# Expert blocks in an order that the chip makes from the token counts, with the second blocks of the two largest experts run on weights still in the ring

## The chip, the cores and the metric

The kernel runs on one core of a Trainium2 chip. The metric is the device time of one execution, in microseconds (us); lower is better. The engines are named as in the profile: PE is TensorE (PEld its weight loads), DVE is VectorE, ACT is ScalarE, POOL is GpSimd, SP is SyncE, which here only issues transfers.

## The reference

A two-part transformer stack over 512 tokens of width 1024, all in float32. The last layer but the final norm is a mixture of experts, and only that part is touched:

```python
def moe_ffn(x, router_w, router_b, w_gu, b_gu, w_down, b_down):
    logits = (xt @ router_w + router_b).astype(jnp.float32)
    top_logits, top_idx = lax.top_k(logits, TOP_K)          # 4 of 32 experts for each token
    gates = jax.nn.softmax(top_logits, axis=-1)
...
        hmid = xt[tok] @ w_gu[e] + b_gu[e]                   # 1024 -> 2048
        glu = jnp.minimum(hmid[:, 0::2], SWIGLU_LIMIT)
        lin = jnp.clip(hmid[:, 1::2], -SWIGLU_LIMIT, SWIGLU_LIMIT)
        act = glu * jax.nn.sigmoid(SWIGLU_ALPHA * glu) * (lin + 1.0)
        return act @ w_down[e] + b_down[e]                   # 1024 -> 1024
...
    y = jnp.einsum("tk,tkd->td", gates.astype(x.dtype), y_slots[slot_of].reshape(n_tok, TOP_K, D))
```

With the inputs of this case the reference's router sends these numbers of tokens to experts 0 to 31 (sum 2048):

```
13 29 105 42 49 66 34 31 44 103 152 37 130 40 66 84 39 41 111 31 98 32 45 50 71 49 124 86 55 57 103 31
```

Thirteen experts have more than 64 tokens. Two have more than 128: expert 10 (152) and expert 12 (130).

## The kernel before

Everything up to the router is a long unrolled program and stays as it is. What follows is `experts`: routing (`out_norm_and_route`), then `first_blocks`, `extra_blocks` and `combine_and_finish`, each a block in which the five engines run their own streams and which ends with a barrier.

**A step of `first_blocks`** handles up to 128 tokens of one expert, and there are 32 steps, j = 0 to 31, in the order of the expert's number. The token rows are fetched by index (POOL, `fetch_rows`), turned by PE (`turn_rows`: the first half before the activations are turned, the second half after), multiplied into the up weights, activated on DVE and ACT, turned again and multiplied into the down weights. ACT stores the result to `expert_rows`. PE ends a step with `find_tokens` (L3559), which prepares the step three later; its row in the trace marks the end of a step.

There are three ways to do the arithmetic. With 64 tokens or fewer a step is **half** (`up_half`, `down_half`): plain float32 matmuls with 64 columns of weights of PE, two of them side by side. With more it is **parted** (`up_parted`, `down_parted`): ACT rounds each weight quarter to its high part, DVE makes the low part, and three fast products replace the float32 one; the low part is written over the weights in the ring (`T.w_low[slot]`), so the weights are used up. Only step 0 can be done **whole** (`up`, `down`): plain float32 matmuls with 128 columns. Which branch is taken is read on each engine from the count of the step (`is_half`, a register loaded from memory, L4198).

**Weights.** An expert has six units of 2 MB: four of the up matrix, two of the down matrix. They lie in a ring of eight slots; SP issues the load of a unit as soon as the unit that had its slot is used (`unit_used`, L4183), so at most one and a third experts are ahead.

**The loop.** Steps 0 to 3 and 28 to 31 are written out, steps 4 to 27 are a hardware loop of six rounds of four steps (`in_rounds`, `Fori` at L4166).

**Second blocks.** If an expert has more than 128 tokens, the rest are done in `extra_blocks`, a loop over 15 possible blocks of which `count` are taken (two here). Each loads its expert's six units again, except that the first one's are issued at the end of `first_blocks` (L4194). It selects its rows from all 512 with 64 matmuls (`gather`, L3665) and then does a half or whole block. DVE finds which experts need one (`Extras.find`, `find_jumps`, `fill`, `find_rows`), in `first_blocks` during steps 0 to 3.

`combine_and_finish` then fetches four result rows for each token (POOL, L4666), sums them with the gates, norms and stores.

Of the kernel before, what the change touches and what calls it, by code (L numbers as in the profile page):

```python
# [5 lines left out]
ALU = mybir.AluOpType  # L6
# [8 lines left out]
P = 128  # L15
# [1006 lines left out]
def mlp(k, i, gain, clear_rows=False):  # L1022
# [15 lines left out]
    with ExitStack() as ctx:  # L1038
# [19 lines left out]
        with k.block() as block:  # L1058
# [35 lines left out]
            def _(act):  # L1094
                if clear_rows:
                    act.wait_ge(k.pool_made.sem, k.pool_made.at(1))
                for n, (u, is_up, j) in enumerate(order):
                    k.round_unit(act, u + 1)
                    if clear_rows:
                        rows = k.rows[3 * n:min(3 * n + 3, BLOCKS)].rearrange("b p d -> p b d")  # L1100
                        act.dma_start(rows, zero[:, :, :].broadcast_to([P, rows.shape[1], D])).then_inc(k.rows_cleared, 16)
# [2362 lines left out]
BLOCKS = EXPERTS + MOST_EXTRA  # L3464
# [3 lines left out]
SLOTS = 8  # L3468

# [32 lines left out]
class Experts:  # L3502


    def __init__(self, k, name, tables, one_by_one):
# [6 lines left out]
        self.loaded = [signal(f"loaded{r}") for r in range(SLOTS)]  # L3512
        self.sel_ready = signal("sel_ready")
        self.index_full = signal("index_full")
        self.index_ready = signal("index_ready")
        self.fetched = [signal(f"rows_fetched{r}") for r in range(2)]
# [16 lines left out]
    def make_sel(self, dve, j, par):  # L3533
# [4 lines left out]
        for t in range(TT):  # L3538
            ins = dve.tensor_scalar(T.sel[:, par, t, :], T.iota[:, :], T.place[:, t, bass.ds(j, 1)], None, ALU.is_equal)
# [95 lines left out]
    def save_act(self, act, j):  # L3635
        k, T = self.k, self.tables
        act.wait_ge(self.act_turned, 2 * j + 2)
        act.activation(T.actT[:, :, :].rearrange("p (b f) s -> p b (f s)", b=2), k.psum[:, 4:6, :], ACT.Copy)\
           .then_inc(self.actT_ready, 2)
# [33 lines left out]
    def up(self, pe, j, home, xg, par):  # L3673

        k, T = self.k, self.tables
        for pair in range(2):
            for r in range(2):
                w = home.wait(pe, 2 * pair + r)
                for g in range(2):
# [4 lines left out]
                    for c in range(HALF_K):  # L3684
                        pe.matmul(bank, xg[:, HALF_K * r + c, :], w[:, c, g * 512:(g + 1) * 512],
                                  start=(r == 0 and c == 0), stop=False)
# [101 lines left out]
    def down(self, pe, j, home, par):  # L3788
        k, T = self.k, self.tables
        self.wait_for_down(pe, j)  # L3790
        for r in range(2):
            w = home.wait(pe, 4 + r)
            for half in range(2):
                bank = k.psum[:, 6 + half, :]
                cols = slice(half * 512, (half + 1) * 512)
                for c in range(HALF_K):
                    pe.matmul(bank, T.actT[:, HALF_K * r + c, :], w[:, c, cols], start=(r == 0 and c == 0), stop=False)
# [207 lines left out]
def experts(k):  # L4005

    with ExitStack() as ctx:
# [3 lines left out]
        T.place = k.sb("moe_place", [P, TT, BLOCKS], ctx=ctx)  # L4011
        T.iota = k.sb("moe_iota", [P, P], ctx=ctx)
# [5 lines left out]
        T.count = k.sb("moe_count", [P, EXPERTS], I32, ctx=ctx)  # L4018
# [7 lines left out]
        T.index = k.sb("moe_index", [P, EXPERTS], I32, ctx=ctx)  # L4026
# [9 lines left out]
        with ExitStack() as inner:  # L4036
# [21 lines left out]
            first_blocks(k, base, T, extras, later)  # L4058
# [4 lines left out]
class Extras:  # L4063
# [4 lines left out]
    def __init__(self, k, T, ctx):  # L4068
        self.k, self.T = k, T
        self.known = k.ctx.enter_context(k.nc.semaphore("extras_known"))  # L4070
        self.flag = k.sb("extra_flag", [P, ROUNDS - 1, EXPERTS], ctx=ctx)
# [18 lines left out]

    def find(self, dve):
# [5 lines left out]
        step(ins)  # L4097
        dve.memset(self.zero[:, :], 0.0)
# [18 lines left out]
    def fill(self, dve, t):  # L4117
# [5 lines left out]
        k.dve.step(dve, self.look_up(dve, self.cand[:, 0], T.place[:, t, EXPERTS:BLOCKS]))  # L4123

    def find_jumps(self, dve):
# [5 lines left out]
        step(dve.tensor_tensor(self.jump[:, 1, :], order[:, 0, :], T.ids[:, :], ALU.subtract))  # L4131
        step(dve.tensor_scalar(self.jump[:, 1, :], self.jump[:, 1, :], float(EXPERTS - 1), float(P), ALU.add, ALU.mult))
        step(dve.tensor_tensor(self.jump[:, 2:, :], order[:, 1:, :], order[:, :-1, :], ALU.subtract))
# [19 lines left out]
def first_blocks(k, E, T, extras, later):  # L4153
# [3 lines left out]
    PER_ROUND = 4  # L4157
    rounds = EXPERTS // PER_ROUND
    k.unit_rounded.passed(len(k.units))
    k.unit_split.passed(len(k.units))  # L4160
    with k.block() as block:
        def in_rounds(eng, step):

            for b in range(PER_ROUND):
                step(0, b, b, True, False)
            with eng.Fori(1, rounds - 1) as i:  # L4166
                for b in range(PER_ROUND):
                    step(i, b, PER_ROUND * i + b, False, False)
            for b in range(PER_ROUND):
                step(rounds - 1, b, PER_ROUND * (rounds - 1) + b, False, True)  # L4170

        @block.sync
        def _(sp):
            def step(i, b, j, first, last):
                if last and b == PER_ROUND - 1:
                    return
# [565 lines left out]
```

## Time and profile before

| what | value |
|---|---|
| median of 3 runs | 3099.53 us (3092.92 to 3102.09) |
| time of the profiled execution | 3098.87 us |
| its span, first to last instruction | 3097.1 us |
| mean granted TensorE clock | 0.935 of full speed |
| `first_blocks` from PE's first expert matmul to its last (1894.2 to 2948.3) | 1054.1 us |
| `extra_blocks`, from there to PE's last expert matmul (3044.1) | 95.8 us |
| from there to the end | 53.0 us |

A time in the trace is a start in us from the span's start, then a duration. "Idle before" in brackets is how long the engine stood still ahead of the row, and what released it; "issue" there means that nothing in the profile was waited for. A row of a queue (PEldq, ACTq, DVEq, SPq) is work of the engine's sequencer, not of the engine.

### The profile page before, as it was taken

How to read it: one execution, taken by the hardware profiler on the slowest of the kernel's cores; microseconds unless marked ns; L12 is line 12 of the kernel's file. 1: busy time of each engine (PE TensorE's matmuls, PEld its weight loads, DVE VectorE, ACT ScalarE, POOL GpSimd, SP SyncE). 2: the span in 40 equal slices, each digit the busy share in tenths (PEclk: the TensorE clock that was granted, in tenths of full speed). 3: DMA queues.
4: the chain of work that ended last, by engine and by line, in shares of the span. 5: the costliest groups of instructions: out<-in, count | busy, mean ns of one | idle time of the engine just before them, and what ended most of it. 6: DMA issues, size and time to landing. Idle time of an engine off the chain costs nothing. (4 is left out here: it accounts for less than half of the span.)

```text
span 3097.1 us, 35668 instructions
## 1 busy us (share of the span) xinstructions
PE 2741.5 (89%) x13162; PEld 1970.5 (64%) x13163; DVE 1614.4 (52%) x2447; ACT 1047.0 (34%) x1464; POOL 193.8 (6%) x213
## 2 busy tenths in 40 slices
PE   7877999999999899999966876998989998899962
PEld 6655778888878788888754663553655455455530
DVE  4864545444555544446855536652855454464413
ACT  4444443322224432233333231330634233343301
POOL 0530000000000000000012130000000000000002
PEclk9988999999999999999976787999999999999986
DMA  3110314444233132322210038999999999999974
GB/s 131 58 51 28 109 62 177 171 169 183 101 120 111 66 116 82 109 82 71 103 60 1 1 122 329 404 414 414 413 385 380 361 412 370 414 412 395 415 291 151
DMA packets 192096, 638.46 MB, mean 206 GB/s; under 512 B 12413, under 2 KB 18204, under 8 KB 191522
## 3 DMA queue, kind: packets, MB, share of 16 engines
q1 hardware_dynamic: 173856, 579.61, 48.7%
q10 hardware_dynamic: 11106, 39.11, 3.2%
q0 software_dynamic: 6912, 16.68, 1.4%
q8 instruction: 151, 2.47, 0.3%
q14 instruction: 71, 0.58, 0.1%
HBM read 600.61 MB, written 43.25 MB: 208 GB/s over the span
## 5 line engine op out<-in xcount | busy, mean ns | idle before, releaser
L91 DVE TENSOR_TENSOR unit_low<-unit_whole,unit_high 128x4096 fp32r<-128x4096 f32 (+3 forms) x95 | 287.8, 3035 | 174.8 <-ACT unit_high L88 172.9
L669 PE MATMUL psum<-tokens_high,unit_high 128*128 128x512 f32 (+2 forms) x1016 | 372.5, 367 | 4.4 <-PEq L865 1.6
L669 PE MATMUL psum<-tokens_high,unit_low 128*128 128x512 f32 (+2 forms) x1016 | 368.7, 363 | 0.0
L669 PE MATMUL psum<-tokens_low,unit_high 128*128 128x512 f32 (+2 forms) x1016 | 368.6, 363 | 0.0
L88 ACT ACTIVATE unit_high<-unit_whole 128x4096 fp32r<-128x4096 f32 (+2 forms) x65 | 225.8, 3474 | 374.2 <-PE psum L669 291.3
L91 DVE TENSOR_TENSOR moe_low<-ring_slot,moe_w_high 128x1024 fp32r<-128x1024 f32 x228 | 266.7, 1219 | 19.4 <-ACT moe_w_high L88 18.4
L88 ACT ACTIVATE moe_w_high<-ring_slot 128x1024 fp32r<-128x1024 f32 x228 | 236.5, 1055 | 61.4 <-PE psum L3875 60.4
L3698 PE MATMUL psum<-ring_slot,hT 128*64 128x512 f32 x1136 | 251.9, 594 | 0.0
L669 PEld LDWEIGHTS psum<-tokens_high,unit_high 128*128 128x128 f32 (+1 forms) x1016 | 191.0, 188 | 37.9 <-DVE unit_low L91 4.0
L669 PEld LDWEIGHTS psum<-tokens_low,unit_high 128*128 128x128 f32 (+1 forms) x1016 | 191.1, 188 | 31.6 <-issue 1.6
L669 PEld LDWEIGHTS psum<-tokens_high,unit_low 128*128 128x128 f32 (+1 forms) x1016 | 191.0, 188 | 30.6 <-issue 0.2
L669 PE MATMUL psum<-unit_high,hidden_high 128*128 128x512 f32 x512 | 199.7, 390 | 0.0
L669 PE MATMUL psum<-unit_high,hidden_low 128*128 128x512 f32 x512 | 199.4, 389 | 0.0
L669 PE MATMUL psum<-unit_low,hidden_high 128*128 128x512 f32 x512 | 199.4, 389 | 0.0
L3741 DVE TENSOR_SCALAR moe_glu<-psum 128x256 f32<-128x256 f32 x42 | 17.8, 425 | 324.4 <-PE psum L3704 232.7
L3698 PEld LDWEIGHTS psum<-ring_slot,hT 128*64 128x64 f32 x1136 | 83.5, 137 | 148.9 <-issue 147.7
L3726 PE MATMUL psum<-ring_slot,moe_actT 128*64 128x512 f32 x640 | 155.8, 641 | 9.7 <-ACT moe_actT L3766 9.7
L1147 DVE TENSOR_TENSOR x_residual<-psum,x_residual 128x512 f32<-128x512 f32 x128 | 84.4, 687 | 117.7 <-PE psum L669 117.7
L3870 PE MATMUL psum<-moe_w_high,moe_xg_high 128*128 128x512 f32 x312 | 131.1, 420 | 0.0
L3755 ACT ACTIVATE moe_sig<-moe_glu 128x256 f32<-128x256 f32 x42 | 17.5, 416 | 316.0 <-DVE moe_glu L3741 316.0
L3871 PE MATMUL psum<-moe_low,moe_xg_high 128*128 128x512 f32 x312 | 122.1, 391 | 0.0
L1137 DVE SCALAR_TENSOR_TENSOR hT<-psum,hidden_relu 128x512 f32<-128x512 f32 x64 | 43.8, 689 | 147.3 <-ACT hidden_relu L1109 147.3
(646 smaller groups left out, 4908.9 us busy)
## 6 DMA issues: line engine op xcount, KB each, us to landing
ring_slot<-in_moe_w_gu SPq DMA_DIRECT2D x118, 2048.0 KB, 19.4
ring_slot<-in_moe_w_down SPq DMA_DIRECT2D x60, 2048.0 KB, 20.5
unit_whole<-in_moe_w_gu SPq DMA_DIRECT2D x18, 2048.0 KB, 16.9
unit_whole<-in_w_up SPq DMA_DIRECT2D x16, 2048.0 KB, 7.5
unit_whole<-in_w_down SPq DMA_DIRECT2D x16, 2048.0 KB, 7.7
expert_rows<-zero_row ACTq DMA_DIRECT2D x15, 1536.0 KB, 5.3
unit_whole<-in_moe_w_down SPq DMA_DIRECT2D x8, 2048.0 KB, 19.7
unit_whole<-in_w_in SPq DMA_DIRECT2D x5, 2048.0 KB, 7.7
```

Of the source, the lines that this page charges most:

```text
L88: return act.activation(self.high, self.whole, ACT.Copy)
L91: return dve.tensor_tensor(self.low, self.whole, self.high.bitcast(F32), ALU.subtract)
L669: ins = pe.matmul(bank, a, c, start=(first and m == 0), stop=(last and m == len(parts) - 1))
L1137: dve.scalar_tensor_tensor(out=hidden[j % 2].whole[:, b, :], in0=bank, scalar=0.0, in1=relu[:, h % 2, :], op0=ALU.max, op1=ALU.mult)\
L1147: dve.tensor_tensor(x, bank, x, ALU.add).then_inc(k.bank_free.sem, 1)
L3698: ins = pe.matmul(banks[g], xg[:, c, 0:HALF], w[c // HALF_K][:, c % HALF_K, g * 512:(g + 1) * 512], start=(c == 0), stop=False)
L3726: ins = pe.matmul(banks[g], T.actT[:, c, 0:HALF], w[c // HALF_K][:, c % HALF_K, g * 512:(g + 1) * 512], start=(c == 0), stop=False)
L3741: dve.tensor_scalar(T.glu[:, pair, :], bank[:, :, 0], 7.0, None, ALU.min).then_inc(self.glu_ready, 2)
L3755: act.activation(T.sig[:, pair, :], T.glu[:, pair, :], ACT.Sigmoid, scale=1.702).then_inc(self.gate_ready, 2)
L3870: pe.matmul(banks[g], a.high[:, f, :], w.high[:, cols], start=(first and q == 0), stop=False)
L3871: pe.matmul(banks[g], a.high[:, f, :], w.low[:, cols], start=False, stop=False)
```

## The change

1. **Order.** DVE ranks the 32 experts by token count (`put_in_order`, new) and makes three tables over 34 steps: the expert of a step (`T.order`), the count (`T.count`) and the column of the placement table (`T.column`). The rank that stands at each step is a fixed list, `RANKS`, which POOL writes with 34 memsets of one column. Expert 0 is always at step 0. Every engine that needs an expert's number reads it from `T.order` by a register load (`expert_at`), DVE also the column (`column_at`).
2. **Second blocks.** The largest expert is at steps 2 and 3, the second largest at 29 and 30; 3 and 30 do its tokens from 128 on, with the weights already in the ring, so SP issues no load for them. Both are done by the branch without parts: first blocks whole, since they have over 64 tokens, second ones half. `extra_blocks` is left for experts beyond these two or beyond 256 tokens; each of its blocks loads its weights itself, and nothing is issued ahead for it.
3. **Steps.** Steps 0 to 4 and 29 to 33 are written out, and 5 to 28 are the loop of six rounds of four.
4. `expert_rows` has 49 blocks for 47; the last of the 16 transfers that clear it in the first MLP writes four blocks for two.

With the token counts above, the order on the chip is (expert:tokens; step 0 first):

```
0:13 21:32 10:128 10:24 31:31 | 26:124 28:55 18:111 23:50 | 2:105 25:49 30:103 4:49 | 9:103 22:45 20:98 8:44 |
27:86 3:42 15:84 17:41 | 24:71 13:40 14:66 16:39 | 5:66 11:37 29:57 6:34 | 12:128 12:2 19:31 7:31 1:29
```

The core of the diff:

```diff
-BLOCKS = EXPERTS + MOST_EXTRA
+SECONDS = 2
+BLOCKS = EXPERTS + SECONDS + MOST_EXTRA
+STEPS = EXPERTS + SECONDS
...
+PER_ROUND = 4
+ROUND_LAST = EXPERTS // PER_ROUND - 1
+AT_SECOND = (3, STEPS - 4)
+RANKS = [EXPERTS - 1, 26, 0, 0, 27] + [r for m in range(12) for r in (2 + m, 14 + m)] + [1, 1, 28, 29, 30]
...
+def in_steps(eng, step):
+
+    for q, b, kind in ((0, 0, "first"), (1, 1, "parted"), (2, 2, "whole"), (3, 2, "whole"), (4, 3, "parted")):
+        step(Step(q, 0, b, kind))
+    with eng.Fori(1, ROUND_LAST) as i:
+        for b in range(PER_ROUND):
+            step(Step(PER_ROUND * i + b + 1, i, b, "parted"))
+    for q, b, kind in ((0, 0, "whole"), (1, 0, "whole"), (2, 1, "parted"), (3, 2, "parted"), (4, 3, "parted")):
+        step(Step(STEPS - 5 + q, ROUND_LAST, b, kind))
...
+        home = T.actT[:, :, :].rearrange("p (b f) s -> p b (f s)", b=2)
+        ins = act.activation(home[:, 0], k.psum[:, 4, :], ACT.Copy)
+        if counted:
+            ins.then_inc(k.unit_rounded.sem, PARTED + 1)
+        act.activation(home[:, 1], k.psum[:, 5, :], ACT.Copy).then_inc(self.actT_ready, 2)
...
+    def put_in_order(self, dve):
+
+        k, T = self.k, self.T
+        step = lambda ins: k.dve.step(dve, ins)
+        flat = self.prod[:, :, :].rearrange("p a b -> p (a b)")
+        more = flat[:, 0:EXPERTS * EXPERTS].rearrange("p (a b) -> p a b", b=EXPERTS)
+        here = flat[:, 0:STEPS * EXPERTS].rearrange("p (a b) -> p a b", b=EXPERTS)
+        keys = self.order[:, 0:EXPERTS]
+        step(dve.scalar_tensor_tensor(out=keys, in0=T.counts[:, :], scalar=float(EXPERTS), in1=T.ids[:, :], op0=ALU.mult,
+                                      op1=ALU.add))
+        step(dve.memset(keys[:, 0:1], -1.0))
+        step(dve.tensor_tensor(more, keys.unsqueeze(1).broadcast_to([P, EXPERTS, EXPERTS]),
+                               keys.unsqueeze(2).broadcast_to([P, EXPERTS, EXPERTS]), ALU.is_gt))
+        step(dve.reduce_sum(T.rank[:, :], more, AX))
+        for i, of in enumerate((T.ids, T.counts)):
+            step(dve.tensor_tensor(here, T.rank[:, :].unsqueeze(1).broadcast_to([P, STEPS, EXPERTS]),
+                                   T.ranks[:, :].unsqueeze(2).broadcast_to([P, STEPS, EXPERTS]), ALU.is_equal))
+            step(dve.tensor_tensor(here, here, of[:, :].unsqueeze(1).broadcast_to([P, STEPS, EXPERTS]), ALU.mult))
+            step(dve.reduce_sum(T.by_step[:, i, :], here, AX))
...
+        step(dve.tensor_copy(T.count[:, :], T.by_step[:, 1, :]))
+        for i, at in enumerate(AT_SECOND):
+            ins = dve.memset(T.by_step[:, 0, at:at + 1], float(BLOCKS - SECONDS + i))
+        step(ins)
+        dve.tensor_copy(T.column[:, :], T.by_step[:, 0, :]).then_inc(self.ordered, 1)
+        dve.wait_ge(self.ordered, 1)
+        for i, at in enumerate(AT_SECOND):
+            e = dve.value_load(T.order[0:1, at:at + 1], min_val=0, max_val=EXPERTS - 1)
+            column = BLOCKS - SECONDS + i
+            ins = dve.tensor_scalar(T.place[:, :, column:column + 1], T.place[:, :, bass.ds(e, 1)], float(P), None, ALU.subtract)
...
+        step(dve.scalar_tensor_tensor(out=self.flag[:, 0, :], in0=T.rank[:, :], scalar=float(SECONDS), in1=self.flag[:, 0, :],
+                                      op0=ALU.is_ge, op1=ALU.mult))
...
-            sp.wait_ge(extras.known, 1)
-            e = sp.value_load(T.ints[0:1, 1:2], min_val=0, max_val=EXPERTS - 1)
-            for n in range(PER_EXPERT):
-                E.unit_used(sp, EXPERTS - 1 if n >= 2 else EXPERTS - 2, (n - 2) % PER_EXPERT, True)
-                sp.dma_start(ring_view(k, n), expert_unit(k, e, n)).then_inc(later.loaded[n], 16)
...
+            sp.wait_ge(extras.ordered, 1)
+            load(Home(E, 0, 1), 1, (None, 0))
+            load(Home(E, 0, 2), 2, (0, 1))
+            load(Home(E, 0, 3), 4, (1, 3))
+            load(Home(E, 0, 4), 5, (3, 4))
+            with sp.Fori(1, ROUND_LAST) as i:
+                for b in range(PER_ROUND):
+                    load(Home(E, i, b + 1), PER_ROUND * i + b + 2, (PER_ROUND * i + b, PER_ROUND * i + b + 1))
+            end = STEPS - 5
+            load(Home(E, ROUND_LAST, 1), end + 2, (end - 1, end + 1))
+            load(Home(E, ROUND_LAST, 2), end + 3, (end + 1, end + 2))
+            load(Home(E, ROUND_LAST, 3), end + 4, (end + 2, end + 3))
...
+                    if s.kind == "parted":
+                        E.up_parted(pe, q, home, xg, par)
+                    else:
+                        E.up(pe, q, home, xg, par, counted)
...
-            E.make_sel(dve, 0, 0)
-            E.make_sel(dve, 1, 1)
+                if s.static and s.q < TT:
+                    extras.find_rows(dve, s.q)
+
+            E.make_sel(dve, 0, 0, 0)
             E.save_tokens(dve, 0)
+            E.make_bias(dve, 0, 0)
+            extras.put_in_order(dve)
+            E.make_sel(dve, 1, 1, column_at(dve, 1))
             E.save_tokens(dve, 1)
-            E.make_sel(dve, 2, 0)
-            E.make_bias(dve, 0, 0)
+            E.make_sel(dve, 2, 0, column_at(dve, 2))
             E.save_gather(dve, 0, 0, 0)
             E.save_gather(dve, 0, 1, 0)
-            E.make_sel(dve, 3, 1)
-            E.make_bias(dve, 1, 1)
+            E.make_sel(dve, 3, 1, column_at(dve, 3))
+            E.make_bias(dve, expert_at(dve, 1), 1)
             extras.find(dve)
             extras.find_jumps(dve)
-            in_rounds(dve, step)
+            in_steps(dve, step)
...
+                if s.static and q in AT_SECOND:
+                    rows = EXPERTS + AT_SECOND.index(q)
+                elif s.kind == "first":
+                    rows = 0
+                else:
+                    rows = expert_at(act, q)
+                counted = s.kind != "first"
+                with act.If(is_half(act, s)):
...
-                with sp.If(b + 1 < count):
-                    following = expert_of(sp, b + 1)
-                    for n in range(PER_EXPERT):
-                        E.unit_used(sp, b, n)
-                        sp.dma_start(ring_view(k, n), expert_unit(k, following, n)).then_inc(E.loaded[n], 16)
-
-            sp.wait_ge(base.down_full, 2 * EXPERTS)
-            sp.dma_start(T.y, k.y_rows.rearrange("(t p) d -> p t d", p=P)).then_inc(T.y_stored, 16)
+                e = expert_of(sp, b)
+                sp.wait_ge(block_free, b + 1)
+                sp.dma_start(T.y, k.y_rows.rearrange("(t p) d -> p t d", p=P)).then_inc(y_loaded, 16)
+                for n in range(PER_EXPERT):
+                    sp.dma_start(ring_view(k, n), expert_unit(k, e, n)).then_inc(E.loaded[n], 16)
+
+            sp.wait_ge(base.down_full, 2 * STEPS)
...
-            act.wait_ge(base.stored, 16 * EXPERTS)
+                act.activation(T.seen[:, :], k.ones[:, 0:1], ACT.Copy).then_inc(block_free, 1)
+            act.wait_ge(base.stored, 16 * STEPS)
+            act.activation(T.seen[:, :], k.ones[:, 0:1], ACT.Copy).then_inc(block_free, 1)
```

Three places of the instruction order are shown, since the steps of the argument rest on them.

DVE, from the start of `first_blocks`, before (`moe_sel` selects a step's tokens, `moe_index` their row numbers, `hT` holds the turned rows of a step, `extra_*` is the search for second blocks):

```order
L3539 TENSOR_SCALAR moe_sel<-moe_iota,moe_place 128x128 x8
L3566 TENSOR_SCALAR moe_index<-psum 128x1 x2
L3539 TENSOR_SCALAR moe_sel<-moe_iota,moe_place 128x128 x4
L3597 COPY moe_bias_ones<-moe_bias_pick 128x128
L3605 TENSOR_TENSOR hT<-psum,feature_vectors 128x512 x2
```

The same place in the changed kernel:

```order
L3575 TENSOR_SCALAR moe_sel<-moe_iota,moe_place 128x128 x4
L3602 TENSOR_SCALAR moe_index<-psum 128x1
L3633 COPY moe_bias_ones<-moe_bias_pick 128x128
L4149 SCALAR_TENSOR_TENSOR extra_order<-moe_counts,moe_ids 128x32
L4151 MEMSET extra_order 128x1
L4152 TENSOR_TENSOR extra_prod<-extra_order 128x1024
L4154 TENSOR_REDUCE moe_rank<-extra_prod 128x32
L4156 TENSOR_TENSOR extra_prod<-moe_rank,moe_ranks 128x1088
L4158 TENSOR_TENSOR extra_prod<-extra_prod,moe_ids 128x1088
L4159 TENSOR_REDUCE moe_by_step<-extra_prod 128x34
```

Here the selection of step 1 moved behind the ranking, which goes on with three more such rows of 1088 columns, seven small ones, two register loads and two small writes to `moe_place`.

ACT, the head of the loop's first step, before (`moe_count` tells half from parted):

```order
L4166 ISA
L4198 TENSOR_LOAD moe_count
L4198 ISA x2
L4311 COMPARE_AND_BRANCH
L3754 REGISTER_ALU
L3755 ACTIVATE moe_sig<-moe_glu 128x256
```

and in the changed kernel:

```order
L3499 ISA
L4262 TENSOR_LOAD moe_order
L4262 ISA x2
L4259 REGISTER_ALU
L4259 TENSOR_LOAD moe_count
L4259 ISA x2
L4416 COMPARE_AND_BRANCH
```

A second register load stands ahead of the branch in every step but 0, 3 and 30.

PE, step 2, the branch for more than 64 tokens, before (one plain unit, then the parted ones):

```order
L3900 MATMUL psum<-ring_slot_54,hT 128x512 x8
L3870 MATMUL psum<-moe_w_high,moe_xg_high 128x512
L3871 MATMUL psum<-moe_low_14813,moe_xg_high 128x512
L3870 MATMUL psum<-moe_w_high,moe_xg_high 128x512
L3871 MATMUL psum<-moe_low_14813,moe_xg_high 128x512
L3875 MATMUL psum<-moe_w_high,moe_xg_low 128x512 x2
```

and in the changed kernel (whole):

```order
L3724 MATMUL psum<-ring_slot_54,hT 128x512 x8
L3724 MATMUL psum<-ring_slot_219,hT 128x512 x4
L3729 MATMUL psum<-moe_bias_parts,moe_bias_ones 128x512
L3724 MATMUL psum<-ring_slot_219,hT 128x512 x4
L3729 MATMUL psum<-moe_bias_parts,moe_bias_ones 128x512
L3724 MATMUL psum<-ring_slot_220,hT 128x512 x8
```

All units of the two first blocks are now plain matmuls; nothing is rounded or split for them.

## Rows read from the trace of the kernel before

**Rows 1.** The page: the granted clock in 40 slices of 77.4 us, in tenths.

```profile
PEclk9988999999999999999976787999999999999986
```

**Rows 2.** Windows: `first_blocks` and `extra_blocks` (engine busy us, granted clock, DMA share, GB/s).

```profile
1894.20:2948.30 1054.10, 972.12 (x4328) 541.18 (x4328) 566.20 (x913) 375.85 (x464) 32.56 (x30) 0.97 1.00 397
2948.30:3044.10 95.80, 64.28 (x340) 33.79 (x340) 11.40 (x30) 5.55 (x13) 0.00 (x0) 0.86 0.53 214
```

**Rows 3.** Who waited for a transfer: PE's only row from 1890 to 2950.

```profile
PE psum L3590 <- DMA hT<-y_rows,moe_index: 11.2, 1, 11.2
```

**Rows 4.** Windows: steps 1 (half), 2 (parted), 4 (half), 5 (parted).

```profile
1924.30:1951.90 27.60, 24.96 (x121) 8.87 (x119) 20.06 (x60) 2.67 (x6) 0.99 (x1) 0.94 1.02 413
1951.90:1993.70 41.80, 40.08 (x164) 28.77 (x163) 35.80 (x55) 25.14 (x27) 1.23 (x1) 0.96 1.02 414
...
2020.80:2046.40 25.60, 23.61 (x121) 9.01 (x119) 5.65 (x17) 2.67 (x6) 0.99 (x1) 1.00 1.02 415
2046.40:2086.70 40.30, 38.45 (x164) 27.53 (x163) 32.40 (x39) 25.13 (x27) 1.23 (x1) 1.00 1.03 415
```

**Rows 5.** PE in order of time: ends of steps 7 and 15.

```profile
2139.56 0.25 PE L3559 MATMUL psum<-moe_token,moe_sel 128*128 128x2 bf16 x4
2143.62 5.35 PE L3698 MATMUL psum<-unit_whole,hT 128*64 128x512 f32 x16 [3.81 <-issue]
...
2433.29 3.65 PE L3698 MATMUL psum<-unit_whole,hT 128*64 128x512 f32 x16 [1.77 <-issue]
```

**Rows 6.** Line L4166, the loop itself, on each engine's queue (ns min/median/max).

```profile
L4166 PEldq COMPARE_BRANCH  x6: 76/6056/6222, 2135.9 to 2827.2; - x6
L4166 ACTq COMPARE_BRANCH  x6: 40/48/50, 2141.8 to 2832.0; - x6
```

**Rows 7.** PE in order of time: a half step's first two weight units.

```profile
2086.88 7.09 PE L3698 MATMUL psum<-ring_slot,hT 128*64 128x512 f32 x32
2093.79 0.39 PE L3704 MATMUL psum<-moe_bias_parts,moe_bias_ones 128*64 128x512 bf16 x2
```

**Rows 8.** Line L4198, ACT's register load of one step's count, window 2212 to 2216.

```profile
L4198 ACTq FUSED_REGOPS  x2: 56/114/172, 2212.7 to 2213.1; - x2
L4198 ACTq SEQ_ASSERT  x1: 27/27/27, 2213.3 to 2213.3; - x1
```

**Rows 9.** DVE in order of time, start of `first_blocks`.

```profile
1875.36 3.08 DVE L3539 TENSOR_SCALAR moe_sel<-moe_iota,moe_place 128x128 bf16<-128x128 f32 x8 [0.60 <-PEq L4458]
...
1891.35 0.69 DVE L3605 TENSOR_TENSOR hT<-psum,feature_vectors 128x512 f32<-128x512 f32 x1 [11.19 <-PE psum L3590]
...
1894.74 1.66 DVE L4103 TENSOR_TENSOR extra_pick<-extra_order,moe_nth 128x1440 f32<-128x1440 f32 x1
...
1900.29 1.65 DVE L4089 TENSOR_REDUCE extra_num<-extra_prod 128x15 f32<-128x1440 f32 x1
...
1908.54 0.43 DVE L3741 TENSOR_SCALAR moe_glu<-psum 128x256 f32<-128x256 f32 x1 [1.13 <-issue]
```

**Rows 10.** PE: the plain unit of a parted step that follows a half one.

```profile
2749.85 7.11 PE L3900 MATMUL psum<-ring_slot,hT 128*128 128x512 f32 x16
2756.44 0.75 PE L3870 MATMUL psum<-moe_w_high,moe_xg_high 128*128 128x512 f32 x1
```

**Rows 11.** ACT: rounding at the same parted step.

```profile
2751.27 0.50 ACTq L3778 DMA_DIRECT2D expert_rows<-moe_o  x1
2752.93 1.06 ACT L3844 ACTIVATE moe_xg_high<-hT 128x1024 fp32r<-128x1024 f32 x1 [1.83 <-issue]
```

**Rows 12.** DVE: the low parts at that step.

```profile
2755.17 5.76 DVE L91 TENSOR_TENSOR moe_low<-ring_slot,moe_w_high 128x1024 fp32r<-128x1024 f32 x5
```

**Rows 13.** Line L4335, the second-block loop's empty rounds, window 3046 to 3056.

```profile
L4335 PEldq COMPARE_BRANCH  x13: 214/214/222, 3046.2 to 3055.1; - x13
```

**Rows 14.** POOL in order of time: the first fetch of result rows.

```profile
3056.64 0.96 POOL L4666 DMA_INDIRECT unit_whole<-expert_rows,moe_row  x1 [189.49 <-PEq L4660]
```

**Rows 15.** DVE in order of time: its first row of `extra_blocks`.

```profile
2951.91 0.88 DVE L3546 TENSOR_SCALAR moe_sel_whole<-moe_iota,moe_place 128x128 f32<-128x128 f32 x4 [14.16 <-issue]
```

More of the change, by code:

```diff
@@ L4057, in experts @@
             later = Experts(k, "extra", T, True)
[L4058 removed]
+            first_blocks(k, base, T, extras)
             extra_blocks(k, later, T, base)
@@ L4204, in _, with step @@
             pool.wait_ge(T.y_stored, 16 * TT)
-            for j in range(EXPERTS):
-                E.fetch_rows(pool, j)
+            for q in range(STEPS):
+                E.fetch_rows(pool, q)
         @block.tensor
         def _(pe):
-            def step(i, b, j, first, last):
-                half = is_half(pe, j)
-                home = Home(E, i, b)
-                par = b % 2
+            def step(s):
+                if s.static and s.q == 1:
+                    pe.wait_ge(extras.ordered, 1)
+                half = is_half(pe, s)
+                q, home, par = s.q, s.home(E), s.par
@@ L4228, in step @@
                 with pe.Else():
[L4229 to L4234 removed]
+                    if s.kind == "parted":
+                        E.down_and_turn_parted(pe, q, home)
+                    else:
+                        E.turn_act(pe, q)
@@ L4235, in step @@
+                if s.has(1):
+                    E.turn_rows(pe, q + 1, 1, 1 - par, saved=q + 3 if s.has(2) else STEPS)
                 with pe.If(half):
-                    E.down_half(pe, j, home, par, parted)
+                    E.down_half(pe, q, home, par, counted)
                 with pe.Else():
-                    if parted:
-                        E.down_parted(pe, j, home, par)
-                    else:
-                        E.down(pe, j, home, par)
-                if not (last and b >= 1):
-                    E.find_tokens(pe, j + 3, 1 - par)
+                    if s.kind == "parted":
+                        E.down_parted(pe, q, home, par)
+                    else:
+                        E.down(pe, q, home, par, counted)
@@ L4283, in step @@
+                if s.has(4):
+                    E.make_sel(dve, q + 4, par, column_at(dve, q + 4))
+                if s.static and s.q == 0:
                     for t in range(TT):
@@ L4323, in first_blocks @@
+                    E.save_down(act, q, rows)
+            in_steps(act, step)
     k.stored.passed(16)
```

234 lines of the change are left out of this document (123 added, 111 removed).

## The prediction

> **What bounds the kernel now.** I read the page's line of clocks first: PE is at nine tenths in all slices of the expert stage but its first and the last two, so no long stretch is lost to a slow clock [rows 1]. Then windows by stage. `first_blocks` takes 1054.1 us with PE busy for 972 and the transfers at 397 GB/s, a DMA share of 1.00; `extra_blocks` takes 95.8 us with the DMA at 0.53 and PE often still [rows 2]. So in the long stage two things look full at once, and the first question is which of them sets the pace. The waits answer it: PE waits for a transfer once, for the first token rows, and never for a weight [rows 3]. The DMA is full because SP asks for a unit as soon as a slot is free, 1.3 experts ahead.
>
> PE's own time by step is therefore what counts. An undisturbed half step is 25.6 us, an undisturbed parted one 40.3 us [rows 4]. Nineteen of the first and thirteen of the second make 1010 us of the 1054. Six units of 2.1 MB at 397 GB/s are 31.7 us, 5.3 us a unit: more than a half step, less than a parted one, and the mean of both is 33, which is why the ring keeps up.
>
> The remaining 44 us: step 0 takes 30.1 instead of 25.6, since DVE is late (below). At the ends of five loop rounds PE stands still. Ahead of step 8 that is 3.81 us, and the 16 records after it take 5.35 us where half a group of 32 takes 3.5, so some 5.5 in all [rows 5, 7]. It looks like a late weight, but the loop's own branch takes 6056 ns on PE's queue in the median, and 48 on ACT's [rows 6]: PE's instructions come late, at the jump back. The Trainium skill (Runtime: NRT & Kernel Launch, Instruction fetch mechanics) says that a taken branch whose target is outside the two pages held forces a fetch of that page. By that rule the order of the experts cannot mend these gaps. The last 13 us or so are steps at a granted clock of 0.94 to 0.96 that last 1.5 to 2 us longer than their kind, as steps 1 and 2 do [rows 4].
>
> **The change, part by part.** The sum is made against the profiled execution, 3098.87 us (span 3097.1 and 1.8 around it), 0.7 under the median of 3099.53.
>
> *The stage for second blocks goes:* no expert is left for it. From PE's last expert matmul of `first_blocks` to its last of all is 95.8 us [rows 2], with two waits for weights or token rows, the selection by matmul and two half blocks. **-95.8.**
>
> *Two steps come in.* The second blocks have 24 tokens and 2, so both are half steps, and cost what any half step costs whatever it holds: 2 x 25.6 = **+51.2** [rows 4]. They load nothing.
>
> *Two steps change kind.* The first blocks of experts 10 and 12 become whole. In a half step two units take 2093.79 - 2086.88 = 6.9 us, as eight pairs of matmuls side by side [rows 7]. Whole, the 16 run one after the other, and the plain unit of a parted step confirms the rate: 6.6 to 7.1 us for one unit [rows 10]. So three times 6.9 more, 20.7, and some 1.2 for four more transposes, the biases and a longer save: 25.6 + 20.7 + 1.2 = 47.5 against 40.3. **+14.4** for two (bounds 0, if the pace were the parted one's, and 20).
>
> *The start.* Ranking is put in DVE's stream ahead of the selection of step 1. A row of 1440 columns takes 1.66, a reduction of as many 1.65 [rows 9], so 1.15 ns a column: two rows of 1024 and six of 1088 are 9.9 us. Nine small ones at 0.2 make 1.9. A register load runs from 2212.7 to 2213.3 on its queue, 0.6 us [rows 8]; two of them and two small writes are 1.6. In all 13.4 us, from about 1878.6 to 1892. Before, DVE stood still there for 11.19 us, waiting for the token rows [rows 9], and that hides most of it. But PE must find step 1's tokens before it may turn step 0's rows, and behind the ranking stand two selections with a register load each (1.5 us each), a round trip to PE (0.5) and the two products of 0.69: the second ends at 1897.2 instead of 1892.9. PE starts 4.3 late. Then DVE has three more register loads and some five more small rows ahead of its first `moe_glu` at 1908.54, for which PE was already waiting: another 2.7 on step 0. A later load and selection costs step 1 about 1.5. **+8.5** (5 to 13). SP's load of expert 21 also waits for the order, some 14 us later than now, and lands well before step 1 at 1932.
>
> *Loop heads.* The loop still jumps back five times. Of the five gaps now, the one behind a parted step was short, 1.77 instead of 3.81 [rows 5]; in the new order every round ends with a half step. **+2.** A round starts with a parted step, which changes nothing.
>
> *One more register load on ACT* in front of each parted step. All eleven now follow a half step, where ACT is latest: store at 2751.27, `moe_xg_high` at 2752.93 [rows 11], DVE's first low quarter ready at 2755.17 + 1.15 = 2756.3 [rows 12]; PE comes free of the plain unit at about 2756.7 [rows 10]. The cover is 0.4 us, the load 0.6: 0.2 to 0.3 a step, **+3** (0 to 7). On DVE the two new loads of a step fall at its end, ahead of 7 us of idle time or more; SP's one load stands ahead of units that are asked for early. They cost nothing, unless the DMA's lead is gone. The transposes of row halves stay on the two sides of the activations and cost nothing new.
>
> *Slow-clock steps:* 13 us over 31 steps, two steps more: **+1.**
>
> *The tail.* Now PE's last matmul at 3044.1 is followed by 13 empty rounds of the second-block loop, 12 intervals from 3046.2 to 3055.1, 0.74 each [rows 13], and POOL starts at 3056.64 [rows 14], 12.5 us behind. Afterwards there are 15 empty rounds, and they begin about 3.4 us behind PE's last matmul, as DVE's first row at 2951.91 shows [rows 15]: 3.4 + 14 x 0.74 + 1.5 = 15.3. **+2.8.** The reload of `x_residual` (2 MB) is hidden behind them. From POOL's first fetch to the end nothing changes.
>
> *The ring.* A resident expert holds six slots for 73 us, so only two units of the next are ahead when its second block starts. The other four are asked for from 7 us into that half step and take 21 us; they are wanted from 33 us on. In the alternation a pair of steps takes 66 us and its weights 63.5. At the end steps 31 to 33 eat a load in 25.6 us that takes 31.7: of a lead of some 14 us, 12 is used. I take **0**.
>
> *The 34 memsets on POOL* lie in an idle stretch of the router stage, and the larger clearing transfer in the first MLP: 0.
>
> Sum: -95.8 + 51.2 + 14.4 + 8.5 + 2 + 3 + 1 + 2.8 = -12.9, so 3098.9 - 12.9 = **3086 us**.
>
> **The rivals.**
>
> *The alternation gives back the gaps.* If the stops at the loop heads are weights that come late, after short steps have run the ring empty, then strict alternation removes them: 27 us of gaps and slow starts and the +2 go, 3057. For it: the DMA share is 1.00 [rows 2]. Against it: the branch's 6056 ns [rows 6], and no wait for a transfer [rows 3]. The page's rule above says the same as the branch's row.
>
> *Everything small is at its upper bound.* Start 13, ACT's chain 7, whole steps 20: +14 on the sum, 3100: no change that can be measured. For it: each of these chains has little or no cover. Against: all would have to err one way.
>
> *Weights come late behind the resident experts, and the kernel gets slower.* The place is steps 31 to 33, and 4 to 6 at the start. If SP asks later, or a unit takes longer than 5.3 us, the lead of 14 us is not there, and each half step that follows costs 6.1 us more, three at the end and one or two at the start, 18 to 30 us: 3104 to 3116. It decides from about 6.5 us a unit or 15 us of delay. Against it: at 5.3 my account leaves 1 to 2 us over at step 33.
>
> *The second blocks are not the ones taken out* (the ranks disagree with the counts): both stages' costs stand, about 3180. Nothing speaks for it.
>
> **How the numbers follow.** A measurement of this kernel tells 0.3%, 9.3 us, from no change. The sum, with errors of some 6 us: 0.66, of which 0.48 lies below 3090.2. The gaps given back: 0.10. The small terms high: 0.16. Weights late: 0.07, of which 0.05 ends above 3108.8. No second blocks removed: 0.01. Faster is 0.48 + 0.10 = 0.58 and slower 0.06 + some of the high terms' tail, 0.09; the same 0.33. The sum's own range is 3077 to 3096. The range for 8 in 10 reaches down to 3068, which leaves out most of the given-back case, and up to 3104: 3068 to 3104.
>
> **What would show it.** No selection matmuls of a gather, 12 fewer loads of 2 MB; steps 2 and 29 of 46 to 49 us; steps 3 and 30 of 25.6; PE's first expert matmul some 4 us later against the ranking's start; five jumps back of about 6 us; parted steps at 40.5; PE waiting for no weight; POOL's first fetch 15 us behind the last matmul. I am wrong if a parted or half step differs from its kind by over 1 us, if PE stops in steps 31 to 33, or if the loop's branch gets short.

## The result, and the profile after

The change makes the kernel slower: 3122.2 us in the median of six runs (3117.6 to 3128.3) against 3098.9, a ratio of 1.0075 (95% interval 1.006 to 1.0091). The forecast was 3086, and 3068 to 3104 the range. The profiled execution took 3121.7, with a span of 3120.0, 22.9 more than before. All ratios below are to the kernel before, measured beside the run; its median was 3098.9, 3101.7, 3099.7 and 3104.1 us in the four comparisons, so differences between medians of two comparisons are uncertain by some us. One of a_pad's eleven executions fell in a slow state and took 7040 us; its ratio leaves that one out.

Four stretches by windows (span, then PE, PEld, DVE, ACT, POOL busy, granted clock, DMA share, GB/s): the start, a whole step (2) and a half step (3), all from PE's first expert matmul to its last, and the rest.

```profile
1884.00:1904.50 20.50, 2.62 (x22) 2.11 (x23) 16.08 (x38) 0.00 (x0) 2.72 (x2) 0.50 0.81 303
1964.60:2011.90 47.30, 44.94 (x126) 20.76 (x126) 12.14 (x41) 4.53 (x9) 0.99 (x1) 1.00 0.38 150
2011.90:2037.40 25.50, 23.57 (x125) 8.54 (x122) 8.94 (x33) 2.09 (x6) 0.99 (x1) 1.00 0.73 286
1904.50:3057.30 1152.80, 1030.06 (x4447) 538.91 (x4484) 534.20 (x929) 338.91 (x438) 34.27 (x32) 0.96 0.91 356
3057.30:3120.00 62.70, 0.00 (x0) 0.00 (x0) 26.17 (x24) 8.45 (x16) 15.59 (x16) 0.54 0.57 214
```

The work between first and last matmul took 1054.1 + 95.8 = 1149.9 [rows 2] and takes 1152.8, where the sum said 20.0 less than before. From the last matmul to the end it was 3097.1 - 3044.1 = 53.0 and is 62.7. Whole and half steps are as forecast (47.3 and 25.5 us in the second and third row). PE's waits in steps 1 to 33 (us in total, times, longest) show what is not:

```profile
PE psum L3943 <- issue: 46.3, 5, 9.5
PE psum L3752 <- DVE moe_act L3789: 32.5, 20, 2.2
...
PE psum L3913 <- DVE moe_low L91: 1.5, 4, 0.7
```

The first of the five L3943 waits in order of time, the end of step 8 and the head of the next round:

```profile
2197.03 0.41 PE L3772 MATMUL psum<-moe_down_bias_parts,moe_bias_ones 128*64 128x512 bf16 x2
2197.38 0.25 PE L3595 MATMUL psum<-moe_token,moe_sel 128*128 128x2 bf16 x4
2206.70 9.65 PE L3943 MATMUL psum<-unit_whole,hT 128*128 128x512 f32 x16 [9.06 <-issue]
```

PE waits for no weight. The five gaps at the loop heads are 9.1, 9.3, 9.0, 9.4 and 9.5 us; those of before were 3.8, 3.7, 1.8, 3.7 and 3.8, 16.8 together. The branches by line on PE's queue (ns min/median/max): the loop's jump back; the branch at a step's head, which goes over the half form to the parted one, all 55 of L4314 and the one behind the first jump; and the branch over the body of the loop for further blocks.

```profile
L3499 PEldq COMPARE_BRANCH  x6: 67/6754/7096, 2193.8 to 2900.6; - x6
L4314 PEldq COMPARE_BRANCH  x55: 65/309/4992, 1904.1 to 3040.3; - x55
L4314 PEldq COMPARE_BRANCH  x1: 4772/4772/4772, 2201.6 to 2201.6; - x1
L4442 PEldq COMPARE_BRANCH  x15: 214/221/6278, 3061.6 to 3078.3; - x15
```

POOL in order of time, its first fetch of the end:

```profile
3079.86 0.96 POOL L4772 DMA_INDIRECT unit_whole<-expert_rows,moe_row  x1 [89.91 <-PEq L4766]
```

The jump back takes 6.7 us where it took 6.1 [rows 6]. New is the second one behind it: 4.8 us for a branch that elsewhere takes 0.3. While it lasts (2201.5 to 2206.5) the instruction queues show this (packets, MB, share):

```profile
q8 instruction: 1, 0.02, 1.4%
q14 instruction: 2, 0.02, 0.9%
```

One packet on q8, of 16384 bytes. The Trainium skill (Runtime: NRT & Kernel Launch, Instruction fetch mechanics) says that instructions come in blocks of 16 KiB, 256 instructions, and that a taken branch to a target outside the blocks held waits for a fetch. So the theory: the change moved the code, and the border of a block now lies between the loop's head and its parted form. By my count of PE's instructions (a matmul and its weight load as two) the parted form begins 78 behind the head, so this falls to about three in ten placements.

### The profile page after: what moved, and what is told of

It reads as the page before. It is cut to its first block and busy times, and to the rows that moved or that the text cites. A ratio compares the mean times of both kernels' runs of the same rounds, so it can differ in the third digit from the quotient of the medians.

```text
span 3120.0 us, 35789 instructions
## 1 busy us (share of the span) xinstructions
PE 2740.6 (88%) x12937; PEld 1938.5 (62%) x12979; DVE 1582.1 (51%) x2448; ACT 1005.0 (32%) x1425; POOL 196.9 (6%) x249
## 5 line engine op out<-in xcount | busy, mean ns | idle before, releaser
L3739 PE MATMUL psum<-ring_slot,hT 128*64 128x512 f32 x1184 | 262.1, 594 | 0.0
L91 DVE TENSOR_TENSOR moe_low<-ring_slot,moe_w_high 128x1024 fp32r<-128x1024 f32 x200 | 233.3, 1220 | 22.4 <-ACT moe_w_high L88 21.3
L88 ACT ACTIVATE moe_w_high<-ring_slot 128x1024 fp32r<-128x1024 f32 x200 | 207.2, 1055 | 59.5 <-PE psum L3918 58.5
L3767 PE MATMUL psum<-ring_slot,moe_actT 128*64 128x512 f32 x624 | 147.0, 625 | 9.2 <-ACT moe_actT L3807 9.2
L3913 PE MATMUL psum<-moe_w_high,moe_xg_high 128*128 128x512 f32 x264 | 109.3, 414 | 1.7 <-DVE moe_low L91 1.5
L3767 PEld LDWEIGHTS psum<-ring_slot,moe_actT 128*64 128x64 f32 x624 | 50.6, 143 | 93.6 <-issue 89.8
L660 PE MATMUL psum<-unit_high,high_parts 128*128 128x512 f32 (+2 forms) x256 | 99.1, 387 | 10.9 <-DVE low_parts L1997 4.5
## 6 DMA issues: line engine op xcount, KB each, us to landing
unit_whole<-in_moe_w_gu SPq DMA_DIRECT2D x16, 2048.0 KB, 12.2
```

The lines of the kernel that those rows point to most:

```text
L88: return act.activation(self.high, self.whole, ACT.Copy)
L91: return dve.tensor_tensor(self.low, self.whole, self.high.bitcast(F32), ALU.subtract)
L660: ins = pe.matmul(bank, a, c, start=(i == 0 and m == 0), stop=(i == len(products) - 1 and m == len(parts) - 1))
L3739: ins = pe.matmul(banks[g], xg[:, c, 0:HALF], w[c // HALF_K][:, c % HALF_K, g * 512:(g + 1) * 512], start=(c == 0), stop=False)
L3767: ins = pe.matmul(banks[g], T.actT[:, c, 0:HALF], w[c // HALF_K][:, c % HALF_K, g * 512:(g + 1) * 512], start=(c == 0), stop=False)
L3913: pe.matmul(banks[g], a.high[:, f, :], w.high[:, cols], start=(first and q == 0), stop=False)
```

## The experiments

**Only the place of the code.** Instructions that are never executed move all that follows. They stand in the branch of step 0 that is not taken (expert 0 has 13 tokens), 200 waits in a_pad and b_pad and 512 in a_pad_page, two to an instruction:

```diff
                 with pe.Else():
                     E.wait_for_up(pe, q)
+                    if s.kind == "first":
+                        for _ in range(200):
+                            pe.wait_ge(extras.ordered, 1)
```

> The changed kernel, with some 100 instructions more on PE's queue in the branch of step 0 for more than 64 tokens, which is not taken here (two waits stand in one instruction, so 200 waits). Nothing more is executed; only the place of all that follows in PE's instructions is moved. Theory 1 (page places): in the changed kernel, at the head of each of the five rounds, the jump back (6.7 to 7.1 us on PE's queue) is followed by a branch over the half form to the parted form (L4314), and that takes another 4.6 to 5.0 us with an instruction fetch of 16384 bytes in it, because the parted form lies in another block of 16384 bytes than the head. The padding moves both into one. Then the branch at the head takes 0.3 us, the gaps at the heads fall from 9.0-9.5 to 3.7 us, and the kernel gains 5 x 5.4 = 27: some 3095. Theory 2 (order): a jump back into a parted step behind a half step costs 9 us because of what the queue did before; no change, 3122. Theory 3 (weights late, seen as issue): no change, 3122.

> The kernel before, with the same 100 instructions more in the branch of step 0 that is not taken. By my count of PE's instructions this puts the border between two blocks of 16384 bytes between the loop's head and its parted form. Theory 1 (page places): the three heads at which a parted step begins a round (steps 12, 20, 24) get gaps of 9 us instead of 3.7, the half ones (8, 16) stay: +16, 3115. Theory 2 (order of kinds) and theory 3 (weights): no change, 3099.

> The changed kernel with exactly 256 instructions more (16384 bytes, 512 waits) in the branch of step 0 that is not taken, where the padded kernel had 100. Every later instruction then has the same place within its block of 16384 bytes as in the changed kernel. Theory 1 (page places): the branches of 4.6 to 5.0 us at the heads and the gaps of 9.0 to 9.5 are back, 3122. Rival: any instructions ahead of the loop remove them; gaps of 3.7 and 3107, as in the padded kernel.

a_pad: 3106.7 us, ratio to before 1.0013 (1.0002 to 1.0025). The two branches on its queue:

```profile
L3499 PEldq COMPARE_BRANCH  x6: 67/6038/6309, 2192.2 to 2887.4; - x6
L4314 PEldq COMPARE_BRANCH  x55: 65/217/939, 1902.0 to 3026.4; - x55
```

Its waits:

```profile
PE psum L3943 <- issue: 18.7, 5, 4.0
PE psum L3913 <- DVE moe_low L91: 8.3, 8, 3.0
PE psum L3739 <- DMA ring_slot<-in_moe_w_gu: 2.4, 1, 2.4
```

b_pad: 3112.1 us, 1.0033 (1.002 to 1.0046), and its line L4218 is the branch at a step's head:

```profile
L4166 PEldq COMPARE_BRANCH  x6: 76/6094/6264, 2131.1 to 2835.4; - x6
L4218 PEldq COMPARE_BRANCH  x51: 65/220/5536, 1890.7 to 2939.4; - x51
```

Its waits, the parted steps' plain unit first and then the half steps':

```profile
PE psum L3900 <- issue: 26.6, 3, 9.4
PE psum L3698 <- issue: 5.5, 2, 3.8
```

a_pad_page: 3124.6 us, 1.0071 (1.0054 to 1.0088), the branch at the head and the wait:

```profile
L4314 PEldq COMPARE_BRANCH  x55: 65/313/4661, 1903.2 to 3041.7; - x55
```

```profile
PE psum L3943 <- issue: 45.8, 5, 9.4
```

With 100 dead instructions the second branch falls from 5.0 to under 1 us and the gaps from 46.3 to 18.7. With 256 both are back. The kernel before, which had the luck, loses it: its three parted heads have 8.9 us each (26.6), its two half ones are as they were. That cost it 10.4 us in the median, where +16 was expected; in the traces PE's time from the end of step 0 to its last matmul grows by 10.3 (1119.8 to 1130.1) for 15.3 us of longer gaps. Theories 2 and 3 said no change in a_pad and b_pad, and are out; so is the thought that any instructions ahead of the loop would do. A period of 256 instructions, as the Trainium skill has it in the section named, fits these three placements (0, 100 and 256 more); no other was tried.

The packets of q8 show the fetch itself. In the changed kernel, a_pad_page and b_pad each of the 13 second branches of 4.0 to 5.5 us has one packet of 16384 bytes that starts while it lasts, the first at 2203.8 in the branch from 2201.6 to 2206.4. In a_pad none starts between the end of the jump back and the first matmul behind it.

a_pad gained 15.5 us between the medians, not 27 (18.4 if each is taken from the kernel before beside it). The two profiled executions differ by 15.6 too; 3.5 of that lies ahead of step 1, and steps 1 to 33 hold 11.9. They take 1120.3 us in the changed kernel (windows):

```profile
1937.00:3057.30 1120.30, 1002.09 (x4335) 528.61 (x4370) 507.36 (x873) 336.13 (x433) 33.28 (x31) 0.97 0.91 357
```

The same stretch of a_pad, and its steps 14 and 16:

```profile
1933.50:3041.90 1108.40, 1007.79 (x4333) 529.55 (x4369) 507.42 (x874) 336.15 (x433) 33.39 (x31) 0.98 0.92 361
2385.30:2410.80 25.50, 23.47 (x119) 8.94 (x117) 5.84 (x17) 2.58 (x6) 0.99 (x1) 1.00 0.96 357
2451.50:2478.50 27.00, 24.85 (x119) 9.09 (x117) 5.84 (x17) 2.58 (x6) 0.99 (x1) 0.94 0.99 378
```

Gaps -27.6; PE, now earlier, waits for DVE's low quarters 6.8 us more, for activations 1.5 more and once 2.4 for a weight; and the same matmuls are busy 5.7 us longer, because more steps run in part at the lower of the two clocks: 27.0 us at a granted 0.94 against 25.5 at 1.00. Together -11.2 of -11.9. With its heads as short as those of before, the changed kernel is still not faster than before: +5.0 us, ratio 1.0013.

**Only the order.**

```diff
-RANKS = [EXPERTS - 1, 26, 0, 0, 27] + [r for m in range(12) for r in (2 + m, 14 + m)] + [1, 1, 28, 29, 30]
+RANKS = [EXPERTS - 1, 26, 0, 0, 27] + [r for m in range(12) for r in (14 + m, 2 + m)] + [1, 1, 28, 29, 30]
```

> The changed kernel with one thing swapped in the table of ranks: in each pair the half step comes first and the parted one second, so steps 4, 5, 7, ... are half and 6, 8, ... 28 parted. PE's instructions stand where they stood. Every round now begins with a half step (no branch over the half form at the head) and ends with a parted one. Theory 1 (page places): only the jump back is left, as at step 16 of the kernel before, which also lay between a parted and a half step: gap 1.8 instead of 9.3, no branch of 4.8 us. Five times 7.5 is 37; the clock took back half of such a gain in the padded kernel, so 3122 - 20 to 37 = 3085 to 3102. Rival (weights): the two half steps 4 and 5 one after the other eat the lead of the loads, and PE waits for a weight in them, up to 12 us; then 3097 to 3114.

3097.6 us, 0.9992 (0.9981 to 1.0003). The gaps are 3.5 us on average (2.3 to 4.4; the row below holds a sixth wait, 0.5), and PE waits for no weight in steps 4 and 5. No branch at a head is long:

```profile
L4314 PEldq COMPARE_BRANCH  x55: 65/225/452, 1901.5 to 3017.9; - x55
```

```profile
PE psum L3739 <- issue: 18.2, 6, 4.4
```

A head whose half form follows it needs no branch; so a table of numbers alone brings 24.6 us, to the time of before. The gaps are larger than the 1.8 expected: that a jump back behind a parted step is short, as at one head of the kernel before, is no rule. Why was not followed up. The rival, late weights, is out.

**No loop.** The same rounds written out on all engines, in the changed kernel (a_flat) and in the one before (b_flat):

```diff
-    with eng.Fori(1, ROUND_LAST) as i:
+    for i in range(1, ROUND_LAST):
```

> The changed kernel with the loop over rounds 1 to 6 written out on all engines: the same instructions in the same order, no jump back. Theory 1: the five gaps of 9.3 us go almost wholly, since PE's instructions then come one after the other; what stays is the short taken branches over the forms not used. 3122 - 46 = 3076, parted steps of 40.5 to 42.5 throughout. If the ring of weights is the true bound (theory 3), the gaps come back as waits of PE for a DMA and the time stays above 3105.

> The kernel before with the same loop written out. Its five gaps are 3.8, 3.7, 1.8, 3.7 and 3.8 us, and with the slow clock behind them some 22 us: 3077. Beside the changed kernel written out it shows what the change is worth without the loop: by the sum on record (-12.9, less the +2 of the heads) the changed one should be 15 us faster; by what the traces show of the tail (POOL starts 22.6 us behind PE's last matmul instead of 15.3) some 8 us faster. If both are equal within 3 us, another term of the sum is wrong too.

a_flat: 3070.3 us, 0.9893 (0.9879 to 0.9907). b_flat: 3082.2, 0.9933 (0.992 to 0.9946). In a_flat PE has no gap of the kind left; with them goes the last reserve of the loads, and step 33 waits 2 us for a weight:

```profile
PE psum L3752 <- DVE moe_act L3789: 33.9, 20, 3.1
PE psum L3918 <- DVE moe_actT_low L3987: 11.6, 11, 1.1
...
PE psum L3739 <- DMA ring_slot<-in_moe_w_gu: 2.0, 1, 2.0
```

Without the loop the change is worth 12.0 us, between the 15 of the sum on record and the 8 expected from the tail; both kernels come out some 5 us off their own expectation (3076 and 3077), in opposite directions. So the worth of the change depends on what it is compared in: +23.3 us as it was placed, +5.0 with good heads (a_pad), -12.0 without loop. The place of the code is the largest part of this, not all of it. From a_pad to a_flat steps 1 to 33 fall from 1108.4 to 1071.5 us, twice the 18.7 of gaps: the matmuls are busy 8.5 us less (1007.8 to 999.3), and PE waits 6.1 less for DVE's low quarters and 2.5 less at L3767 for ACT. From before to b_flat the time from the end of step 0 to PE's last matmul falls by 16.6 only, about its gaps. The loop costs the changed kernel, which has a parted step behind every jump, more than the old one.

**The end.** An if around the loop for further blocks:

```diff
+            with eng.If(count > 0):
                 with eng.Fori(0, MOST_EXTRA) as b:
                     with eng.If(b < count):
                         body(b)
```

> The changed kernel with an if around the whole loop for further blocks (count > 0), on all engines, so that with no block left it is jumped over once instead of 15 empty rounds. Theory: POOL now starts 22.6 us behind PE's last matmul: 4.3 us to the loop, 6.3 us for the first branch over the loop's body, which fetches, 14 intervals of 0.74 and some 1.5 to the barrier. With the if one branch with a fetch stays: 22.6 - 14 x 0.74 = 12.2 us behind, 3122 - 10.4 = 3112. If another engine or the reload of x_residual (issued at 3060, some 7 to 13 us) holds the barrier, POOL starts not before 3073 and the gain is at most 6.

> The changed kernel with its round loop written out and the if around the loop for further blocks. Written out alone POOL starts 30.8 us behind PE's last matmul, since two branches of that loop take 7.1 and 7.4 us. With one of them left and no rounds: some 12 us behind, 3070 - 18 = 3052. If the barrier waits for the reload, 3056.

a_tail: 3112.2 us, 1.0039 (1.0027 to 1.0051), 10.0 less. PE's last matmul ends at 3056.1; PE's one branch there, and POOL's first fetch:

```profile
L4441 PEldq COMPARE_BRANCH  x1: 5987/5987/5987, 3060.1 to 3060.1; - x1
```

```profile
3067.29 0.96 POOL L4773 DMA_INDIRECT unit_whole<-expert_rows,moe_row  x1 [78.56 <-PEq L4767]
```

That is 11.2 us behind PE's last matmul instead of 22.6, and 12.2 was expected. The reload of `x_residual` does not hold it. a_flat_tail: 3051.2, 0.9846 (0.9833 to 0.9859), 19.1 less than a_flat, where two branches over the body took 7.1 and 7.4 us (the row has the longest) and POOL started 30.8 us behind:

```profile
L4442 PEldq COMPARE_BRANCH  x15: 214/214/7359, 3001.1 to 3026.0; - x15
```

**ACT's register load**, moved from ahead of a step's work to just ahead of its store:

```diff
-                    rows = expert_at(act, q)
+                    rows = None
+                home_row = lambda: expert_at(act, q) if rows is None else rows
...
-                    E.save_down(act, q, rows)
+                    E.save_down(act, q, home_row())
```

> The changed kernel written out, with ACT's register load of the block number moved from ahead of a step's work to just ahead of its store. If the load is what makes a parted step 40.7 to 40.9 instead of 40.3, undisturbed parted steps become 40.3, and 12 of them give 4 to 5 us: 3066. If the 0.4 comes from elsewhere (a form that is placed across a block of instructions), no change, 3070.

3061.5 us, 0.9873 (0.9857 to 0.989), 8.8 less than a_flat. Two parted steps of a_flat at the full clock:

```profile
2254.70:2295.80 41.10, 38.76 (x165) 27.65 (x166) 32.40 (x39) 25.24 (x28) 1.23 (x1) 1.00 1.02 412
2524.30:2565.20 40.90, 38.77 (x162) 27.52 (x164) 32.41 (x39) 25.16 (x27) 1.23 (x1) 1.00 1.02 413
```

One of this kernel, and one with a stretch at the lower clock:

```profile
2190.60:2230.90 40.30, 38.43 (x167) 27.63 (x166) 32.45 (x39) 25.07 (x28) 1.23 (x1) 1.00 1.03 415
2256.20:2298.10 41.90, 40.18 (x165) 28.75 (x164) 32.55 (x39) 25.16 (x27) 1.23 (x1) 0.96 1.02 414
```

From one step's `find_tokens` to the next, the seven of a_flat at the full clock are 40.5 to 41.0 us, 40.7 on average, the six of this kernel 40.2 or 40.3: 0.5 a step of the 0.6 that the load takes [rows 8], 5 to 6 us for eleven. So the load has next to no cover. The rest of the 8.8 goes with the clock: of the half steps 1 to 30, seven of a_flat last over 26.3 us at a granted clock of 0.94 and two of this kernel (0.89 and 0.94), and PE's matmuls in steps 1 to 33 are busy 996.0 us instead of 999.3. That the clock fell less often because of the edit is not shown.

**All three together.**

> The three edits together on the changed kernel: the round loop written out, the if around the loop for further blocks, ACT's register load moved to just ahead of the store. By themselves they gave -52, -19 and -9 us (the last two against the kernel written out). If they add up: 3051 - 9 = 3042. If the clock takes part of it back, as it did in the padded kernel: 3042 to 3048.

3045.1 us (3042.0 to 3050.2), 0.9819 (0.9801 to 0.9836): 59 us less than before in the same comparison, and 6.1 less than a_flat_tail (8.4 by the two ratios), where 9 were expected if the parts add up. Steps 1 to 33 take 1063.0 us, those of a_flat_act 1062.9.

## Why the prediction was wrong

The account, on the two profiled executions: forecast -12.9, measured +22.9, so 35.8 to explain.

- **The loop heads, the step that failed.** "+2", and "A round starts with a parted step, which changes nothing": it is 46.3 - 16.8 = +29.5, 27.5 of the 35.8. I took the price of a jump back from [rows 6] and stopped there. That the head's own branch may need a fetch too, and that this hangs on where the code stands, was in the rule that I cited; I used it only to say that the order cannot mend the gaps, and a_swap shows that it can. The kernel before had three parted heads with 3.7 us, which I read as the rule; b_pad shows that it was a placement. With a good placement the term is right: in a_pad the heads have 18.7, 1.9 more than before. The time is not: 3106.7 us lies outside the range too, so the failed step does not carry the whole miss, and the items below have the rest.
- **The tail, mis-sized.** "+2.8", 15.3 behind the last matmul; it is 22.6, and the stretch to the end 9.7 longer instead of 2.8: +6.9. Before, two rounds of that loop ran and no branch over the body in the 13 empty ones behind them took over 0.22 us [rows 13]. Afterwards the first one takes 6.3 us, the length of a fetch; a_tail, which takes one branch instead of 15, gives back 10.0.
- **ACT's register load, mis-sized.** "+3 (0 to 7)". Written out, it costs 0.5 a parted step, and in the changed kernel those at the full clock are 40.6 to 40.8 against 40.3: 4 to 6 for eleven, inside the bounds. The cover of 0.4 us worked out from [rows 10 to 12] is not there, or 0.1.
- **Ahead of the change**, in code that it hardly touches (the memsets on POOL and one clearing transfer), the profiled execution is 6.3 us later (PE's first product of step 0's selection at 1884.0 instead of 1877.7). Over the twelve profiles of this study that moment lies between 1873.7 and 1884.0, in the three of the old order between 1875.1 and 1882.3, so it scatters in both; what differs is the granted clock of single stretches, as from 274 to 331 us, first before:

```profile
274.00:331.00 57.00, 40.99 (x218) 34.53 (x219) 26.93 (x40) 24.62 (x46) 0.00 (x0) 0.76 0.18 65
```

and after, with 0.68:

```profile
274.00:331.00 57.00, 41.05 (x200) 34.50 (x198) 25.07 (x40) 23.14 (x44) 0.00 (x0) 0.68 0.18 65
```

- **The start**: 4.3 late and 2.7 more on step 0; measured 3.9 (20.4 instead of 16.5 us to the first expert matmul) and 2.4. Right.
- **The stage that goes, the steps that come and the two whole ones**: half steps 25.5, whole ones 47.3 where I had 47.5. Right. **The ring**: PE waits for no weight. Right here, but the reserve is nearly used up: in step 33 of a_pad, a_flat and a_flat_act one wait of 1.3 to 2.4 us appears.
- What is left is 35.8 - 27.5 - 6.9 - 6.3 = -4.9, in which ACT's 1 to 3 too many stand; so 6 to 8 us went the other way, and they are not assigned.
- **The rivals.** The gaps given back: the stops were no late weights, as argued, but 0.10 for a gain stood beside nothing for a loss at the same place. Weights late: it did not happen. The slower side was given 0.09 for the wrong mechanism. What the text named as the sign of a wrong forecast, a loop branch that changes, was sought in the wrong direction: longer, not shorter.

## What to carry to other kernels

In a loop with branches on PE, look not only at the jump back but at each branch behind it, and at where the code stands: dead instructions ahead of the loop are a cheap test, and 100 of them moved this kernel by 15 us down and the one before by 10 up. A change that moves code should be compared at more than one placement, or with the loop written out, before its own worth is judged; here the same change came out at +23, +5 and -12 us. Once this loop's rounds were written out, empty rounds and small loads on an engine without cover were the next to go, and they added up nearly in full.

## What the runs showed of the hardware

A jump back behind a half step costs PE 5.9 to 7.1 us on its queue, behind a parted one 3.6 to 6.1, and a second fetch right behind it 4.0 to 5.8 us more (the longest in a_tail), although the one packet of q8 above takes 1.4% of 16 engines over 5 us, 1.1 us. Nearly all other branches at a step's head take up to 0.5 us, some 0.6 to 3.0. Between two jumps back q8 brings 10 to 12 packets of 16384 bytes in every round (before, after and a_pad), so the round's code is fetched anew each time. On ACT's queue the same loop's branch takes 0.05 us. And a stop that is taken away from PE is not gained in full: in a_pad 5.7 of 27.6 us came back as matmuls at the lower clock, 6.8 as waits for DVE.
